# Sixteen heads' four-tap short convolution: from channel by token with transposes to token by channel with shifted copies in SBUF

## The reference, cut to what matters

```
proj = rmsnorm(x) @ w_in
qkv, z_a, ... = split(proj)
qkv = silu(causal_depthwise_conv(qkv, w_conv_qkv))   # 4 taps over tokens, one weight per tap and channel
q, k, v = split(qkv)                                  # 16 heads of 128 channels each
q, k = l2norm(q), l2norm(k)
A  = (k * beta) @ k^T * decay ;  qk = q @ k^T * decay # per head, chunks of 64 tokens
```

## Time and profile before

| | |
|---|---|
| median of 3 runs | 2143.05 us (2142.75 to 2144.01) |
| the profiled execution | 2143.54 us; its span 2141.7 us, granted clock 0.998 |
| PE busy | 2109.3 us (98%) |
| DVE busy | 1484.5 us (69%) |
| ACT busy | 1240.1 us (58%) |
| POOL busy | 333.7 us (16%) |
| DMA in the heads' stage (49 to 418 us) | 0.72 of 16 engines, 207 GB/s |

### The profile page before, as it was taken

One profiled execution on the slowest core, in us unless ns is written; L12 is line 12 of the kernel. 1 busy time (PEld: TensorE's weight loads), 2 busy tenths in 40 slices (PEclk: granted clock), 3 DMA queues, 4 the chain that ended last, 5 costly groups with the idle time before them and its releaser, 6 DMA issues.

```text
span 2141.7 us, 28914 instructions
## 1 busy us (share of the span) xinstructions
PE 2109.3 (98%) x9933; PEld 1744.8 (81%) x9933; DVE 1484.5 (69%) x2750; ACT 1240.1 (58%) x2391; POOL 333.7 (16%) x451
## 2 busy tenths in 40 slices
PE   7999999999999999999999999999999999999998
PEld 5888888888888888888888877887888888888886
DVE  5877777788999986668675555643666745456666
ACT  5666666677777765457555544553454555555543
POOL 1111111147566642010000000000000000000000
PEclk9999999999999999999999999999999999999999
DMA  8867676678877866666776655565665556554462
GB/s 264 240 196 211 199 203 192 195 214 239 261 195 215 236 205 219 197 238 214 261 272 240 236 201 190 192 196 162 209 227 202 188 180 197 186 168 138 157 216 99
DMA packets 430547, 441.79 MB, mean 206 GB/s; under 512 B 27489, under 2 KB 302049, under 8 KB 427745
## 3 DMA queue, kind: packets, MB, share of 16 engines
q1 hardware_dynamic: 412880, 382.81, 57.6%
q0 software_dynamic: 7680, 36.05, 5.0%
q10 hardware_dynamic: 9872, 21.50, 2.7%
HBM read 413.02 MB, written 27.28 MB: 206 GB/s over the span
## 4 chain that ended last, share of the span: by engine, by line
PE 88%; DVE 8%; issue 1%; ACT 1%; SPq 1%; DMA 0%; POOL 0%; DVEq 0%; POOLq 0%; ACTq 0%
PE pair L460 26%; PE pair L462 26%; PE pair L461 26%; DVE w_lo L441 3%; DVE QB L1065 2%; PE QA L1472 1%; PE RA L1488 1%; PE RA L622 1%; SPq L397 1%; DMA raw<-in_w_in_dram 0%; PE QB L1557 0%; PE RA L798 0%; PE RA L1714 0%; PE RB L1714 0%; POOL acc_p L1034 0%
## 5 line engine op out<-in xcount | busy, mean ns | idle before, releaser
L441 DVE TENSOR_TENSOR w_lo<-raw,w_hi 128x512 fp32r<-128x512 f32 x1368 | 920.6, 692 | 416.4 <-ACT w_hi L434 415.5
L434 ACT ACTIVATE w_hi<-raw 128x512 fp32r<-128x512 f32 x1368 | 828.6, 625 | 469.7 <-PE pair L462 458.3
L460 PE MATMUL pair<-w_hi,in_hi 128*128 128x512 f32 x2336 | 935.9, 401 | 6.9 <-DVE w_lo L441 4.1
L462 PE MATMUL pair<-w_hi,in_lo 128*128 128x512 f32 x2336 | 912.0, 390 | 0.0
L461 PE MATMUL pair<-w_lo,in_hi 128*128 128x512 f32 x2336 | 910.7, 390 | 0.0
L460 PEld LDWEIGHTS pair<-w_hi,in_hi 128*128 128x128 f32 x2336 | 439.5, 188 | 95.0 <-DVE w_lo L441 5.3
L462 PEld LDWEIGHTS pair<-w_hi,in_lo 128*128 128x128 f32 x2336 | 438.8, 188 | 93.6
L461 PEld LDWEIGHTS pair<-w_lo,in_hi 128*128 128x128 f32 x2336 | 439.6, 188 | 87.1 <-issue 1.0
L1034 POOL TENSOR_TENSOR acc_p<-acc_p,tap 128x256 f32<-128x256 f32 x160 | 184.3, 1152 | 38.5 <-ACT tap L1008 25.1
L1008 ACT ACTIVATE tap<-upad,cwl 128x256 f32<-128x256 f32 x192 | 96.9, 508 | 51.9 <-POOL acc_p L1034 51.0
L1065 DVE SCALAR_TENSOR_TENSOR QB<-upad,cwl,QB 128x256 f32<-128x256 f32 x272 | 119.8, 480 | 0.0
(11 more groups left out here) (401 smaller groups left out, 1864.4 us busy)
## 6 DMA issues: line engine op xcount, KB each, us to landing
raw<-in_w_in_dram SPq DMA_DIRECT2D x512, 256.0 KB, 3.9
raw<-in_w_in_dram SPq DMA_DIRECT2D x80, 1024.0 KB, 5.1
raw<-in_w_out_dram SPq DMA_DIRECT2D x48, 1024.0 KB, 5.0
raw<-in_w_kv_shared_dram SPq DMA_DIRECT2D x24, 1024.0 KB, 5.0
raw<-in_w_br_a_dram SPq DMA_DIRECT2D x16, 1024.0 KB, 6.0
raw<-in_w_br_b_dram SPq DMA_DIRECT2D x16, 1024.0 KB, 6.2
raw<-in_w_mem_kv_dram SPq DMA_DIRECT2D x16, 1024.0 KB, 4.9
raw<-in_w_ple_gate_dram SPq DMA_DIRECT2D x16, 1024.0 KB, 5.0
```

Of the source, the lines that this page charges most:

```text
L434: act.activation(piece(blk, q)[0], raw[:, u, q % UK], ACT.Copy).then_inc(hi_ready[u], 1)
L441: dve.tensor_tensor(lo, raw[:, u, q % UK], hi.bitcast(F32), ALU.subtract).then_inc(lo_ready[u], 1)
L460: pe.matmul(o, xh, wh, start=(q == 0), stop=False)
L462: mm = pe.matmul(o, xl, wh, start=False, stop=(q == KC - 1))
```

## The change

The short convolution stays with tokens on partitions. Both groups of six transposes, the copies around them and the per-partition taps go. The weights of a head (4 taps by 384 channels) are broadcast over all partitions into `wt` by one transfer per head on SP's queue, in two buffers. With P0 = `proj`, the four taps are made as: `qkv_old` = w1 P0 (DVE, hs 3), `by_one` = P0 shifted down by one token (three transfers on ACT's queue after the tanh of hs 1: 112 partitions, 15 partitions and 1), `qkv_sum` = w0 `by_one` (DVE, hs 11), `qkv_old` += `qkv_sum` (DVE, hs 12), `by_two` = `qkv_old` shifted by two tokens (three more transfers, ACT hs 14), and on POOL `qkv_new` = w3 P0 + w2 `by_one` in three operations. DVE adds the two (hs 23), ACT takes the tanh (hs 24), DVE gates it into `tok` (hs 26), ACT squares it (hs 28). Each of these is one operation of 768 columns. The scores part stands later in all lists: DVE's scaling at hs 5 instead of 1, PE at hs 15 and 18 instead of 6 and 9, ACT's `kq` copies at hs 16 instead of 7, DVE's `ap` at hs 20 instead of 11, the stores at hs 25 instead of 16. SP's loop over heads is written out, and each head's weights are asked for after its block. Buffers that shared memory with the new ones are cleared later on POOL.

```diff
-    conv_in = sb("conv_in", [P, 3, SHORT - 1 + S + 1])
-    conv = sb("conv", [P, 3, S])
-    conv_th = sb("conv_th", [P, 3, S])
+    qkv_old = sb("qkv_old", [P, TT, QKV])
+    qkv_sum = sb("qkv_sum", [P, TT, QKV])
+    qkv_th = sb("qkv_th", [P, TT, QKV])
...
-    cw = sb("cw", [P, SHORT, 3])
...
+    by_one = sb("by_one", [P, TT, QKV])
+    by_two = sb("by_two", [P, TT, QKV])
+    qkv_new = sb("qkv_new", [P, TT, QKV])
+    qkv_tap = sb("qkv_tap", [P, TT, QKV])
+    wt = sb("wt", [P, 2, SHORT, 3, P])
...
-    def keys_pe(pe, h, hs):
-        if hs == 3:
-            pe.wait_ge(psum_free, BLK_A + h + 1)
-            reach(pe, s["tok_ready"], h)
-            for c in range(3):
-                bank = QB[:, 0:S] if c == 2 else QA[:, c * S:(c + 1) * S]
-                for tile in range(TT):
-                    mm = pe.transpose(bank[:, tile * P:(tile + 1) * P], proj[:, tile, c * P:(c + 1) * P], ident)
-            mm.then_inc(s["qkv_cols"], 1)
-        if hs == 19:
-            pe.wait_ge(s["silu_done"], h + 1)
-            for tile in range(TT):
-                for c in range(3):
-                    mm = pe.transpose((QA, QB)[tile][:, c * P:(c + 1) * P], conv[:, c, tile * P:(tile + 1) * P], ident)
-            mm.then_inc(s["qkv_tokens"], 1)
+    def weight(par, k):
+
+        return wt[:, par, k].rearrange("p c n -> p (c n)").unsqueeze(1).broadcast_to([P, TT, QKV])
+
+    def taps_in_sp(sp, h, par):
+        sp.dma_start(wt[:, par].rearrange("p k c n -> p (k c n)"), t["w_conv_qkv"][h].partition_broadcast(P))\
+          .then_inc(s[f"wt_in{par}"], 16)
+
+    def shift_act(act, to, src, n, done):
+
+        act.dma_start(to[16:P, :, :], src[16 - n:P - n, :, 0:QKV]).then_inc(done, 16)
+        act.dma_start(to[n:16, :, :], src[0:16 - n, :, 0:QKV]).then_inc(done, 16)
+        act.dma_start(to[0:n, 1], src[P - n:P, 0, 0:QKV]).then_inc(done, 16)
 
     def keys_act(act, h, par, hs):
         if hs == 0:
             act.wait_ge(psum_ready, h + 1 + BLK_A)
-            reach(act, s["qkv_cols"], h)
+            reach(act, s["one_in"], 48 * h)
             reach(act, s["z_gated"], h)
+            reach(act, s["taps_on_dve"], 4 * h - 3)
+            reach(act, s["taps_on_pool"], 3 * h - 2)
             act.activation(proj[:, 0], pairs[par][:, 0], ACT.Copy, scale=x_rms[:, 0:1])
             act.activation(proj[:, 1], pairs[par][:, 1], ACT.Copy, scale=x_rms[:, 1:2]).then_inc(psum_free, 1)
         if hs == 1:
             act.wait_ge(psum_free, BLK_A + h + 1)
+            if isinstance(h, int) and h == 0:
+                act.wait_ge(s["pads_ready"], 4)
+            reach(act, s["taps_on_dve"], 4 * h - 2)
+            reach(act, s["taps_on_pool"], 3 * h - 1)
             act.activation(z_th[:, :, :], proj[:, :, 3 * P:4 * P], ACT.Tanh, scale=0.5).then_inc(s["z_tanh"], 1)
-        if hs == 5:
-            act.wait_ge(s["conv_filled"], h + 1)
-            act.wait_ge(s["cw_staged"], h + 1)
-            reach(act, s["qkv_tokens"], h)
-            for c in range(3):
-                ins = act.activation(conv[:, c], conv_in[:, c, 0:S], ACT.Copy, scale=cw[:, 0, c:c + 1])
-            ins.then_inc(tap_done, 1)
+            shift_act(act, by_one, proj, 1, s["one_in"])
...
         if hs == 14:
-            act.wait_ge(tap_done, SHORT * h + SHORT)
-            act.activation(conv_th[:, :, :], conv[:, :, :], ACT.Tanh, scale=0.5).then_inc(s["conv_tanh"], 1)
-        if hs == 20:
-            act.wait_ge(s["qkv_tokens"], h + 1)
-            reach(act, s["tok_scaled"], h)
-            act.activation(tok[:, 0].rearrange("p c n -> p (c n)"), QA[:, 0:3 * P], ACT.Copy)
-            act.activation(tok[:, 1].rearrange("p c n -> p (c n)"), QB[:, 0:3 * P], ACT.Copy)\
-               .then_inc(s["tok_ready"], 1)
-        if hs == 21:
+            act.wait_ge(s["taps_on_dve"], 4 * h + 3)
+            shift_act(act, by_two, qkv_old, 2, s["two_in"])
+        if hs == 24:
+            act.wait_ge(s["taps_on_dve"], 4 * h + 4)
+            reach(act, s["tok_ready"], h)
+            act.activation(qkv_th[:, :, :], qkv_sum[:, :, :], ACT.Tanh, scale=0.5).then_inc(s["conv_tanh"], 1)
+        if hs == 28:
...
-        reach(pool, tap_done, SHORT * h)
         pool.tensor_copy(hst[:, par], head_all[:, bass.ds(h, 1)].rearrange("p a n -> p (a n)"))\
             .then_inc(s["head_staged"], 1)
-        taps = chan[:, CH_SHORT:CH_LONG].rearrange("p (k c h) -> p k c h", k=SHORT, c=3)
-        pool.tensor_copy(cw[:, :, :], taps[:, :, :, bass.ds(h, 1)].rearrange("p k c a -> p k (c a)"))\
-            .then_inc(s["cw_staged"], 1)
+        pool.wait_ge(psum_free, BLK_A + h + 1)
+        pool.wait_ge(s[f"wt_in{par}"], 8 * h + (16 - 8 * par))
+        reach(pool, s["taps_on_dve"], 4 * h)
+        pool.tensor_tensor(qkv_new[:, :, :], proj[:, :, 0:QKV], weight(par, 3), ALU.mult).then_inc(s["taps_on_pool"], 1)
+        pool.wait_ge(s["one_in"], 48 * h + 48)
+        pool.tensor_tensor(qkv_tap[:, :, :], by_one[:, :, :], weight(par, 2), ALU.mult).then_inc(s["taps_on_pool"], 1)
+        pool.wait_ge(s["taps_on_pool"], 3 * h + 2)
+        pool.tensor_tensor(qkv_new[:, :, :], qkv_new[:, :, :], qkv_tap[:, :, :], ALU.add).then_inc(s["taps_on_pool"], 1)
...
+        if hs == 7:
 
             dve.wait_ge(s["z_tanh"], h + 1)
             dve.scalar_tensor_tensor(z2[:, :, :], z_th[:, :, :], 1.0, proj[:, :, 3 * P:4 * P], ALU.add, ALU.mult)\
                .then_inc(s["z_gated"], 1)
-        if hs == 4:
-            dve.wait_ge(s["qkv_cols"], h + 1)
-            dve.tensor_copy(conv_in[:, 0:2, SHORT - 1:SHORT - 1 + S], QA[:, :].rearrange("p (c n) -> p c n", c=2))
-            dve.tensor_copy(conv_in[:, 2, SHORT - 1:SHORT - 1 + S], QB[:, 0:S]).then_inc(s["conv_filled"], 1)
-        if hs in (7, 10, 13):
-            k = (hs - 4) // 3
-            dve.wait_ge(tap_done, SHORT * h + k)
-            for c in range(3):
-                ins = dve.scalar_tensor_tensor(conv[:, c], conv_in[:, c, k:k + S], cw[:, k, c:c + 1], conv[:, c], ALU.mult, ALU.add)
-            ins.then_inc(tap_done, 1)
+        if hs == 3:
+            dve.wait_ge(psum_free, BLK_A + h + 1)
+            dve.wait_ge(s[f"wt_in{par}"], 8 * h + (16 - 8 * par))
+            reach(dve, s["two_in"], 48 * h)
+            dve.tensor_tensor(qkv_old[:, :, :], proj[:, :, 0:QKV], weight(par, 1), ALU.mult).then_inc(s["taps_on_dve"], 1)
+        if hs == 11:
+            dve.wait_ge(s["one_in"], 48 * h + 48)
+            reach(dve, s["tok_ready"], h)
+            dve.tensor_tensor(qkv_sum[:, :, :], by_one[:, :, :], weight(par, 0), ALU.mult).then_inc(s["taps_on_dve"], 1)
         if hs == 12:
+            dve.wait_ge(s["taps_on_dve"], 4 * h + 2)
+            dve.tensor_tensor(qkv_old[:, :, :], qkv_old[:, :, :], qkv_sum[:, :, :], ALU.add).then_inc(s["taps_on_dve"], 1)
+        if hs == 13:
             dve.wait_ge(s["z_gated"], h + 1)
             reach(dve, s["ap_stored"], 32 * (h - 1))
             dve.tensor_tensor(ex[:, par, EX_ZS:EX_ZS + S].rearrange("p (t n) -> p t n", t=TT), z2[:, :, :], both(half_g[:, :]),
                               ALU.mult)
-        if hs == 16:
+        if hs == 23:
+            dve.wait_ge(s["two_in"], 48 * h + 48)
+            dve.wait_ge(s["taps_on_pool"], 3 * h + 3)
+            dve.wait_ge(s["taps_on_dve"], 4 * h + 3)
+            dve.tensor_tensor(qkv_sum[:, :, :], qkv_new[:, :, :], by_two[:, :, :], ALU.add).then_inc(s["taps_on_dve"], 1)
+        if hs == 26:
             dve.wait_ge(s["conv_tanh"], h + 1)
-            dve.scalar_tensor_tensor(conv[:, :, :], conv_th[:, :, :], 1.0, conv[:, :, :], ALU.add, ALU.mult)\
-               .then_inc(s["silu_done"], 1)
+            reach(dve, s["tok_scaled"], h)
+            reach(dve, s["norms_summed"], 4 * h)
+            dve.scalar_tensor_tensor(tok[:, :, :, :].rearrange("p t c n -> p t (c n)"), qkv_th[:, :, :], 1.0, qkv_sum[:, :, :],
+                                     ALU.add, ALU.mult).then_inc(s["tok_ready"], 1)
...
     def scores_pe(pe, h, par, hs):
-        if hs == 6:
+        if hs == 15:
...
-        if hs == 9:
+        if hs == 18:
...
-        if hs == 7:
+        if hs == 16:
...
-        if hs == 16:
+        if hs == 25:
...
     def scores_dve(dve, h, par, hs):
-        if hs == 1:
+        if hs == 5:
...
-        if hs == 6:
+        if hs == 5:
             dve.wait_ge(s["decay_exp"], h + 1)
...
-        if hs == 11:
+        if hs == 20:
...
+    def a_buffers_pool(pool):
         pool.wait_ge(s["cols_lo"], KC // 2)
         pool.wait_ge(s["x_ss"], TT)
+        pool.memset(by_one[0:1, 0], 0.0).then_inc(s["pads_ready"], 1)
+        pool.memset(by_two[0:2, 0], 0.0).then_inc(s["pads_ready"], 1)
...
-        with sp.Fori(2, HEADS) as h:
+        sp.wait_ge(s["cols_lo"], KC // 2)
+        sp.wait_ge(s["x_ss"], TT)
+        for h in range(2):
+            taps_in_sp(sp, h, h)
+        for h in range(2, HEADS):
             load_heads(sp, BLK_A + h, COL_A, h)
+            sp.wait_ge(s["taps_on_dve"], 4 * h - 6)
```

(6 more changed lines are left out.)

46 lines of the change are left out of this document (24 added, 22 removed).

## The result

The changed kernel takes 2246.03 us (2245.36 to 2247.82, four runs) beside 2143.39 us for the kernel before on the same chip: a ratio of 1.0479, 95% interval 1.0466 to 1.0492. I had forecast 2172, slower, and a range up to 2187. The sign and the place are right, the size is not: the loss is 103 us instead of 29.

A forecast was written before the change was run, and what follows sets the result against it. The prediction took PE's own list of work to bound the heads' stage, 24.6 us a block. Fifteen blocks 1.4 us longer (21.0) plus 8.0 for the first heads, on 2143.5, gave 2172 us; range 2160 to 2187.

The forecast's parts named there:

- The transposes: Two groups of six on PE per head, 0.67 us each: removal takes a block from 24.6 to 23.3 us without waits.
- PE's place for `kq`: PE needs `kq` at hs 18, 13.5 us after the block's start, counted as half-chunks plus the six remaining transposes.
- A: End of DVE's sum at line 607, from the block's start: 10.5 us without POOL, 13.7 with it; PE waits beyond 11.0.
- DVE's scalings end at 6.3, its mask product waits till 7.1: + 0.8: POOL's second operation, after `by_one` at 5.2 us, runs to 7.1 and holds DVE's mask product: A + 0.8 us.
- the 1.7 behind it: POOL's third operation gets in behind DVE's mask product, 7.4 to 9.1 us: A + 1.7 us.
- The + 0.7 for POOL's first product: POOL's `qkv_new`, 2.2 to 3.9 us, makes DVE's `w_lo` begin at 3.9 instead of 3.2: A + 0.7 us.
- one issue takes 0.33 us, three 1.0: ACT's time to issue a shift's three transfers, ahead of `w_hi` and ahead of the `kq` copies: 1.0 us each time.
- The first heads: Late `wt` for head 0 and POOL's holds: + 6.3 us in block 1, + 1.7 in block 2, together + 8.0.
- The load: DMA engines in the heads' blocks: 1.5 MB added to 5.1 in 26 us, a share of about 0.82, which fits.
- POOL takes nothing: First rival: POOL takes nothing from DVE, A at 10.5, blocks of 23.3 us, 2126 us in all; chance 0.28.
- Late landing: Second rival: `by_one` lands at 8 us or beyond, A about 15.5, block 27.8, total 2200 us; chance 0.09.
- It cancels: Third rival: `by_one` at 4 us and issues cheaper than 0.33, block 24.2 to 24.5, 2143 to 2146 us; chance 0.07.

The follow-up runs named there:

- POOL's product behind: Changed kernel with one added wait: POOL's tap product starts only after DVE's scalings of the head before; 2174.86 us, ratio 1.0149.
- early weights: Changed kernel with head 0's tap weights asked for ahead of the decays on SP's queue; 2235.12, 2235.19, 2236.96 us and one run of 2175.86.
- later scores: Changed kernel with PE's scores at hs 21 instead of 18 and DVE's decay product at hs 24 instead of 20; 2163.13 us, ratio 1.0102.
- the three moves: Changed kernel with second shift behind the key copies, head 0's tap weights first, POOL's tap product behind the scalings; 2135.24 us, ratio 0.9965.
- the later shift: Changed kernel with ACT's second shift at hs 17, behind the `kq` copies, instead of hs 14; 2147.97 us, ratio 1.0021.

## Why the prediction was wrong

**Right.** The transposes: blocks without a wait are 23.4 to 24.0 us, 23.3 as worked out. The chain: PE waits at hs 18, released by ACT, behind the shift, behind line 607. PE's place for `kq`, 13.5 us, also in the wait's size: `kq` comes at 18.4, less 4.9. `by_one` at 5.2 us: POOL starts on it at 5.1.

The block takes 30.7 us for the forecast 26.0. The step that failed first is the price of an issue: it makes the wait before `kq` 1.1 us longer ahead of A and 1.1 us again behind it. The second is the clock, which the sum has no term for: 2.2 to 2.5 us. A third, where POOL holds DVE, was wrong in its place and right in its size by luck.

**Wrong, the step "DVE's scalings end at 6.3, its mask product waits till 7.1: + 0.8", and the 1.7 behind it.** I took the scalings as free of POOL because they have one input, and put the price on the mask product and a `w_lo`. It was the other way round: the scalings lost 3.1 us (the 96 of line 668 have a median of 0.276 and a longest of 1.943 us), the mask product and the `w_lo` behind them nothing. Where POOL's product begins at 6.3, as in the kernel with matmuls in the wait, it is again a scaling that stands, 1.96 us, and the mask product takes its 0.41. The + 0.7 for POOL's first product isn't there either: it ends at 4.2, and the `w_lo` behind it waits for ACT's `w_hi` until 4.3. The same section of the Trainium skill that I cited (SBUF — State Buffer, Who interferes with whom) frees an instruction with one SBUF input only outside the 2-port modes, and says in a bullet further on that `tensor_scalar` can enter a mode that takes the shared pair of ports, and then contends. I had left that condition out. The scalings' 1.9 us beside POOL's product agree with it; no run here shows which mode they were in. The total for the three operations, 3.1 instead of 3.2 us, came out nearly right by this error.

**Wrong, "one issue takes 0.33 us, three 1.0".** The row was that of stores from SBUF to DRAM of one shape. These transfers, between partitions of SBUF, take 0.58 to 0.91 us each in the block shown, 2.1 to 2.2 for three. That is 1.1 us between A and `kq` (A + 3.6 for A + 2.5), and 1.1 more ahead of the first `w_hi`, so that the scalings start at 4.9 instead of 3.8. Put in, in place of the three terms for POOL, these two make the forecast's sum right: A is 10.5 + 1.1 + 3.1 = 14.7 (14.8 measured, for my 13.7), its limit is 13.5 - 3.6 = 9.9 instead of 11.0, and PE waits 4.8 us (4.85 measured). With POOL off the scalings, A is 11.6 and the wait 1.7, as the kernels with POOL's product behind and with POOL cut to one column have it. So the issues alone turn a gain of 1.3 us per block into a loss of 0.6 (25.3 for 24.7), and meeting POOL makes it 6.

**Missing, the clock.** 2.2 to 2.5 us per block, nearly as much as the wait that I had forecast. A wait of 1.66 us left the granted clock at 1.00 in the 2 us stretches behind it; 4.85 us brought it to 0.50, and one of 3.33 us in the kernel with early weights did too. Between them both are seen: one of 2.32 us (POOL cut to one column, at 149.05) left it at 1.00, and behind one of 2.76 us (later scores, at 451.23) it fell to 0.50.

**Missing, that the state feeds itself.** I worked out one block with `by_one` at 4.6 to 6.5 and took the ends for a spread. The cost has steps instead. With the scalings between 4.9 and 6.8 us, `by_one` at up to 6.1 us lets POOL meet two of them (A at 14.8), from 6.2 to 6.4 one (13.2) and from 6.5 to 9.1 none (11.6); from 9.3 on DVE itself waits and is held (15.0 to 15.6). Most kernels are at one of the two levels for nearly all heads; the one with matmuls in the wait changes from head to head. That two early heads decide for the rest is shown by a run. That it is `wt` under way which makes `by_one` late is read from the traces and borne out by the last blocks, where `wt` is absent; no run moved `wt` alone.

**The first heads.** + 13.7 in block 1, not + 6.3. DVE had `wt` at 62.47 instead of 60.6, and behind it the two `w_lo` took 4.52 us and the gating product 2.04, held by POOL's three operations one after the other; PE waited 7.74 us once. The three waits that I forecast there add to 7.6, so the wait was about right. What I left out is behind it: the granted clock is 0.79 and 0.85 in the stretches from 57 to 67 and to 76 us, and ACT starts the next copy late, at 85.26, without having idled. How the rest divides between these two is open. The rows, DVE's and then PE's timeline:

```profile
62.47 0.96 DVE L600 TENSOR_TENSOR qkv_old<-proj,wt 128x768 f32<-128x768 f32 x1 [13.62 <-DMA wt<-in_w_conv_qkv_dram]
63.35 4.52 DVE L448 TENSOR_TENSOR w_lo<-raw,w_hi 128x512 fp32r<-128x512 f32 x2
67.79 2.04 DVE L594 SCALAR_TENSOR_TENSOR z<-z_th,proj 128x256 f32<-128x256 f32 x1
```
```profile
65.69 0.79 PE L467 MATMUL pair<-w_hi,in_hi 128*128 128x512 f32 x1 [7.74 <-DVE w_lo L448]
```

POOL's three are 1.84 us each only when nothing is beside them: `qkv_new` takes 2.64 when it begins with DVE's `qkv_old`, as in the block shown above, and 1.84 when it begins a microsecond later, as with the three moves.

**The load.** By the rows that I used, 1.5 MB on 5.1 in 26 us is a share of 0.88, not 0.82. Measured are 0.87 in blocks of 25.3 us and 0.93 in those of 23.4.

**The rivals.** POOL takes nothing: refuted. But what it was to give, blocks of 23.3 us, is what the later shift gives by another way. Late landing: between 6.5 and 9.1 us, which blocks of 23.4 to 25.3 us bring about, it helps; beyond that it costs what I had worked out for it (A at 15.5, measured 15.0 to 15.6), in three blocks of three kernels. It cancels: refuted, the issues are dearer than 0.33 us and `by_one` never lands before 4.98.

## What to carry to other kernels

Price a DMA issue by a row of the same kind of transfer, and ask what stands behind the issues on that queue: here moving three of them behind two copies was worth 98 us. Look at a wait of TensorE for the clock that it will cost too, and for whether it is long enough to cost it. Where two engines share something and their phase hangs on a DMA's landing time, work out the block with the landing on each side of every edge, and ask which of them the block's own length brings about; a wait on the engine off the path can be the cheapest repair.

## What the runs showed of the hardware that I had not expected

- A POOL operation behind which DVE runs two-input operations back to back isn't held for one of them but for many: 768 columns took 5.7 to 8.8 us instead of 1.9, and with POOL cut to one column such an operation still took 5.6 us (the one at 242.44) for 0.2 to 0.3 otherwise. The earlier trace rows had shown POOL getting in between; here it did so beside the scalings and when it began together with a DVE operation that had waited for the same rows, as at 146.69 above, and otherwise mostly not.
- TensorE's wait of 4.85 us costs 2.2 to 2.5 us more after it has ended, one of 1.66 us about 0.2 (25.3 - 23.4 - 1.66).
- Filling a wait with 4.1 us of useless matmuls made the kernel 45 us faster, and a wait added on GpSimd, which acts in three blocks of its profile, 71 us.
- Transfers that move 1.5 KB take as long to issue, 0.6 us, as those of 336 KB, and those over 14 or 15 partitions longest, 0.8 to 0.9.
